# Two held operands of TensorE at a shifted address: cT by 256 bytes and dT by 384 bytes, in a two-layer hybrid trunk with experts

## The reference

```
for layer in (0, 1):
    h = rms_norm(x, mix_norm[layer])
    a, b, p, gc, gp = split(h @ w_in[layer])              # 1024 -> 3584 columns
    yc = silu(layer_norm(causal_conv31(a * sigmoid(b)))) @ w_conv_out[layer]
    yp = (sliding means of p over 2, 4, 8, 16 tokens - p) @ w_pool[layer] * pool_scale[layer]
    x = x + (sigmoid(gc) * yc + sigmoid(gp) * yp) @ w_out[layer]
    h = rms_norm(x, ffn_norm[layer])
    if layer == 0:  x = x + (silu(h @ w_gate) * (h @ w_up)) @ w_down           # width 2816
    else:           x = x + the two best of 8 experts of the same form, width 3584, weighted
return rms_norm(x, final_norm)
```

## Time and profile before

| what | value |
|---|---|
| median of three runs | 1425.84 us (1425.17 to 1426.02) |
| the profiled execution, its own time | 1425.18 us |
| its span in the profile | 1423.6 us |
| TensorE matmuls / weight loads | 6506 / 6506 |
| TensorE busy | 1409.4 us, 99% of the span |
| mean granted clock of TensorE, share of full speed | 0.998 |
| VectorE, ScalarE, GpSimd busy | 1174.7, 986.9, 207.9 us |
| memory traffic | 445.96 MB, 313 GB/s over the span |

### The profile page before, as it was taken

One profiled execution on the slowest core, in us unless ns is written; L12 is line 12 of the kernel. 1 busy time (PEld: TensorE's weight loads), 2 busy tenths in 40 slices (PEclk: granted clock), 3 DMA queues, 4 the chain that ended last, 5 costly groups with the idle time before them and its releaser, 6 DMA issues.

```text
span 1423.6 us, 18360 instructions
## 1 busy us (share of the span) xinstructions
PE 1409.4 (99%) x6506; PEld 1168.6 (82%) x6506; DVE 1174.7 (83%) x1068; ACT 986.9 (69%) x876; POOL 207.9 (15%) x249
## 2 busy tenths in 40 slices
PE   9999999999999999999999999999999999999997
PEld 7888888888888888888888888888888888888885
DVE  6987544548987998889899898888989989888896
ACT  7765444347765877867877777786787777778674
POOL 6840000005831001001001001000100100100010
PEclk9999999999999999999999999999999999999999
DMA  9656555545548899999999999999999999999990
GB/s 359 222 169 215 178 181 198 183 162 196 175 164 310 283 386 378 371 370 409 375 382 372 390 367 371 388 370 369 412 372 384 370 391 366 371 389 373 366 411 33
DMA packets 197552, 445.96 MB, mean 313 GB/s; under 512 B 8400, under 2 KB 19968, under 8 KB 197504
## 3 DMA queue, kind: packets, MB, share of 16 engines
q1 hardware_dynamic: 192496, 432.57, 80.4%
q0 software_dynamic: 2304, 8.39, 2.2%
q10 hardware_dynamic: 2704, 4.38, 0.9%
HBM read 437.97 MB, written 7.34 MB: 313 GB/s over the span
## 4 chain that ended last, share of the span: by engine, by line
issue 58%; PE 34%; POOL 4%; DVE 2%; ACT 1%; DMA 0%; POOLq 0%; ACTq 0%; DVEq 0%
PE bank L1467 10%; PE bank L1469 10%; PE bank L1468 10%; POOL small L611 2%; POOL gates L614 2%; DVE w_lo L989 1%; POOL sums L621 1%; PE bank L1528 1%; DVE bank L1038 1%; PE bank L1631 0%; PE bank L1593 0%; ACT w_hi L654 0%; PE bank L1763 0%; PE bank L1587 0%; DVE tokA L1104 0%
## 5 line engine op out<-in xcount | busy, mean ns | idle before, releaser
L989 DVE TENSOR_TENSOR w_lo<-raw,w_hi 128x2048 fp32r<-128x2048 f32 x256 | 582.9, 2292 | 134.8 <-ACT w_hi L654 134.6
L654 ACT ACTIVATE w_hi<-raw 128x2048 fp32r<-128x2048 f32 x256 | 488.6, 1913 | 200.2 <-PE bank L1469 199.8
L1467 PE MATMUL bank<-w_hi,dT_hi 128*128 128x512 f32 (+1 forms) x756 | 296.4, 392 | 0.0
L1469 PE MATMUL bank<-w_hi,dT_lo 128*128 128x512 f32 (+1 forms) x756 | 293.2, 388 | 0.0
L1468 PE MATMUL bank<-w_lo,dT_hi 128*128 128x512 f32 (+1 forms) x756 | 292.6, 387 | 0.0
L1467 PE MATMUL bank<-w_hi,cT_hi 128*128 128x512 f32 x492 | 194.3, 395 | 0.0
L1469 PE MATMUL bank<-w_hi,cT_lo 128*128 128x512 f32 x492 | 191.7, 390 | 0.0
L1468 PE MATMUL bank<-w_lo,cT_hi 128*128 128x512 f32 x492 | 191.6, 390 | 0.0
L1469 PEld LDWEIGHTS bank<-w_hi,dT_lo 128*128 128x128 f32 x756 | 142.0, 188 | 29.4
L1467 PE MATMUL bank<-w_hi,hT_hi 128*128 128x512 f32 x416 | 164.4, 395 | 1.1 <-DVE w_lo L1086 1.0
L1468 PEld LDWEIGHTS bank<-w_lo,dT_hi 128*128 128x128 f32 x756 | 142.2, 188 | 28.1
(11 more groups left out here) (256 smaller groups left out, 1865.8 us busy)
## 6 DMA issues: line engine op xcount, KB each, us to landing
raw<-in_moe_w_gate_dram SPq DMA_DIRECT2D x96, 1024.0 KB, 7.5
raw<-in_moe_w_up_dram SPq DMA_DIRECT2D x72, 1024.0 KB, 10.3
raw<-in_moe_w_down_dram SPq DMA_DIRECT2D x72, 1024.0 KB, 8.9
raw<-in_w_in_dram SPq DMA_DIRECT2D x20, 1024.0 KB, 7.1
mix<-in_moe_w_up_dram SPq DMA_DIRECT2D x16, 1024.0 KB, 8.8
gates<-in_moe_w_down_dram SPq DMA_DIRECT2D x16, 1024.0 KB, 11.3
gates<-in_moe_w_up_dram SPq DMA_DIRECT2D x16, 1024.0 KB, 8.8
work<-in_moe_w_down_dram SPq DMA_DIRECT2D x16, 1024.0 KB, 11.5
```

What stands on the lines that cost most here:

```text
L654: act.activation(w_hi[split_place(u, seen.item is not None)][:, 0:width], place[slot][:, 0:width], ACT.Copy).then_inc(hi_ready, 1)
L989: dve.tensor_tensor(w_lo[split][:, 0:width], place[slot][:, 0:width], w_hi[split][:, 0:width].bitcast(F32), ALU.subtract).then_inc(lo_read ...
L1467: nc.tensor.matmul(dst, a_hi, b_hi, start=start, stop=False)
L1469: return nc.tensor.matmul(dst, a_lo, b_hi, start=False, stop=stop)
```

## The change

Buffers are named in another order, and one unused buffer is added. `rw` moves from the end of the list to its front, `vecs` and `items` move from the front to just before `cT`. The bytes ahead of `raw` stay the same (256 + 64 + 64 for 224 + 64 + 32 + 64), so `raw`, `w_hi`, `w_lo`, `hT` and all that lies up to `y_lo` keep their addresses. `cT_hi` and `cT_lo` begin 256 bytes later than before, which is 256 past a multiple of 512. `to_384` adds 128 bytes more, so `dT_hi` and `dT_lo` begin 384 past a multiple of 512, and so do `row_gain`, `ident`, `mean_w` and `mix`; `taps` moves by 384 and the last small buffers by 128. The list now ends at 229288. No instruction is added, removed or moved.

```
@@ -230,9 +230,8 @@
-        vecs = sb("vecs", [P, 56])
+        rw = sb("rw", [P, KD, E])
         small = sb("small", [P, 16])
-        items = sb("items", [P, 8], I32)
         sb("to_512", [P, 16])
         raw = sb("raw", [P, RAW, UNIT])
@@ -252,8 +251,11 @@
         y_hi, y_lo = sb("y_hi", [P, D], F32R), sb("y_lo", [P, D], F32R)
+        vecs = sb("vecs", [P, 56])
+        items = sb("items", [P, 8], I32)
         cT_hi = sb("cT_hi", [P, CC * S], F32R)
         cT_lo = sb("cT_lo", [P, CC * S], F32R)
+        sb("to_384", [P, 32])
         dT_hi = sb("dT_hi", [P, GROUPS * S], F32R)
         dT_lo = sb("dT_lo", [P, GROUPS * S], F32R)
@@ -267,7 +269,6 @@
         taps = sb("taps", [P, 2, 124])
-        rw = sb("rw", [P, KD, E])
```

## The result

The changed kernel takes 1441.21 us (median of four, 1440.66 to 1441.9) against 1425.93 for the kernel before in the same comparison: a ratio of 1.0102, interval 1.0088 to 1.0115, or +15.3 us. The profiled execution has a span of 1439.7 us where it was 1423.6.

A forecast was written before the change was run, and what follows sets the result against it. TensorE's matmul spacing was taken to bound the kernel, everything ahead of it being early. All parts summed to 0 us on the profiled 1425.18 us; with the runs' median 0.66 us higher, the forecast was 1425.8 us, range 1388 to 1450.

The forecast's parts named there:

- Parts 1, 3, 4 and 5: Unchanged instructions; moved ident, mean_w, row_gain; mix as loading place and split source; moved vecs, items, rw, taps: 0 us each.
- part 2: cT 256 and dT 384 bytes on against unmoved streams, 4560 matmuls: spacing stays 226.7 ns, +0 us (bounds -53.4 to +37.8).
- one lost cycle per 16 bytes loaded: Reading of the 13.3 ns extra per large matmul as 32 cycles for a 512-byte held block, wherever the buffers lie.
- the strongest sign: Unsteady steps behind four transposes, ten averaging 231.0 ns and two of 235, with the same buffers as in steady stretches.
- the case without it: The forecast itself: distance has no meaning for the large matmuls, spacing stays 226.7 ns; 1425.8 us, chance 0.40.
- Rival B: Distance 0 is a good place; shifted cT and dT matmuls stay at 231.0 ns, +19.6 us, 1445 us; chance 0.25.
- The objection to it: Argument against the slower side: in the unsteady steps behind the transposes time is shifted, and no address; no size.
- Rival A: Distance 0 is a bad place for cT and dT matmuls; losing half the extra gives -27 us, 1399 us; chance 0.35.
- parts 2 and 3: Estimates for cT and dT matmuls and for transposes and means, both using 1.7 ns extra of a full float32 matmul.
- If an address matters at all, it is by its last 9 bits: In steady stretches, distances of 0 and 512 past a multiple of 1024 cost the same 226.7 ns per step.
- The rule of the Trainium skill: TensorE's two independent read ports let the next held operand load without taking bandwidth from the running matmul: 0 us.

The follow-up runs named there:

- e2_rest_only: The change with cT and dT put back at multiples of 512, only row_gain, ident, mean_w and mix still 384 past one: 1425.84 us, ratio 0.9998 to the kernel before.
- e6_both_256: The change without the 128 bytes of to_384, so cT and dT both at distance 256: 1426.09 us, ratio 1.0000 to the kernel before.
- e3_streams_128: Kernel before with streamed buffers and hT moved to 128 past a multiple of 512, cT and dT unmoved, both at distance 384: 1451.27 us, ratio 1.0175.
- e9_who_meets: Kernel before with test matmuls added behind its end, offsets alternating, then other widths and full float32; alternating offsets gave steps of 228.2 to 230.0 ns; no total given.

## Why the prediction was wrong

**The bound was read rightly.** TensorE's spacing set the end, nothing ahead of it was late, and every ns per matmul showed: step times count, with the counts of the prediction, gives 14.8 us for a median that rose by 15.3. Parts 1, 3, 4 and 5 hold: e2_rest_only and e6_both_256 put all of them together at 0 within 0.1%.

**The step that failed is part 2,** "The value that I take is 226.7, no change". For cT at 256 it is right. For dT at 384 the measured step is 232.4 in an undisturbed stretch, and the part that was put at +0 us is +14.8 us. I had put down the reason for "no change" as one lost cycle per 16 bytes loaded, which fitted two widths of stream and was never tested against the width of the load; held blocks of 96, 64 and 32 columns refute it (230.0 to 231.7 ns where it gives 223.3 to 216.7). Why the spacing depends on the distance stays open. The rows of before held better evidence: the earlier trace rows show steps of up to 235 ns with the same buffers, so the spacing is no constant. The prediction called this the strongest sign that the address could matter and then gave the forecast to the case without it.

**Rival B had the right direction and a close size.** It said that distance 0 is the good place and that a shifted held block would leave the spacing at the mean of the unsteady steps. The spacing does stay unsettled; that this comes from load and stream meeting, as B has it, no run shows, and the steps at 384 are not those behind the transposes. It priced that at 231.0 ns on all 4560 matmuls, +19.6 us; it was 232.4 on the 2784 that hold dT, and nothing on the other 1776. What it lacked is the period: 256 is as good as 0, so one of the two moved buffers cost nothing. The objection to it, that in those rows time is shifted and no address, did not hold it back: both count, as distance 16 shows. The longest step was given as 235 and is 241.

**That the time lies between 1388 and 1450 is luck.** The upper end was to leave out spacings above 232 ns, and the measured one is above it. It is 1441 only because cT, at 256, happened to cost nothing; e3_streams_128, where cT and dT both pay, is at 1451.3, outside.

**Rival A is refuted for these matmuls.** In 17 distances on the 16-byte grid, their repeats up to 480 and four distances off the grid none is below 226.65 ns. The 215.0 ns of the float32 record (215.7 over the 63 steps above, so its extra is nearer to 2.4 than to the 1.7 ns of parts 2 and 3) was reached at no distance. At 256 columns of `F32R` distance 0 is the worse place, by 1.4 ns; the kernel has few such matmuls.

**"If an address matters at all, it is by its last 9 bits"** held as far as tried: the last 8 bits of the distance set the steps.

**The rule of the Trainium skill** ("TensorE: Matmul & The Clock Gate", Part 2: What happens when you issue a matmul), by which loading the next held operand takes nothing from the running matmul, gave 0 us and was wrong here by 15.3. The runs do not show which read takes what from which, so the two ports themselves are not refuted; but a matmul's spacing depends on where the held operand lies against the streamed one, at 512 columns of `F32R`.

## What to carry to other kernels

When matmuls with 128 held columns run back to back at 512 columns of `F32R`, lay held and streamed buffers out so that their addresses differ by a multiple of 256 bytes; every other distance tried here cost 0.7 to 3.3% of each matmul at least at some starts, but for 272, which was tried from one start alone. It shows in no wait of TensorE, only in the distance between starts. For other widths measure: at 256 columns 128 was the better distance. Small buffers named between large ones set this distance by accident, and a few bytes of padding repair it. Where a trace shows that a cost varies from one matmul to the next for the same buffers, don't take the settled value for what a moved buffer will cost, and don't judge a layout by stretches that are all entered in the same way.

## What the runs showed of the hardware that I had not expected

- Spacing of 512-column `F32R` matmuls against distance: 226.7 ns at multiples of 256 bytes, 228.8 to 234.2 at the other multiples of 32, repeating every 256 bytes. The loss at distance 128 was 5.5 ns at 512 columns, 1.1 at 448, 2.2 at 384, 0 at 320 and -1.4 at 256. Full float32 of 256 columns has 215.7 ns per record at 0 and at 128.
- Steps fall into repeating patterns of unequal steps, at 384 one of seven (241, 232, 231, 232, 228, 230, 233) and, in e3_streams_128, another of 229 or 230 and 237 or 238 by turns. At distance 16 two patterns exist, 226.7 and 233.3, in the same kernel.
- At distance 0 with 128 held columns the step is columns / 2.4 plus 13.3 ns at 256, 320, 384 and 512 columns, and plus 16.0 at 448; it doesn't fall with the width of the held block. At distance 128 and 256 columns it is plus 11.9.
- In e9_who_meets the granted clock fell from 1.00 to 0.50 of full speed, the level of 1.2 GHz, at 1513 us, behind 17 us of matmuls with 128 and 64 columns (and 12 us of 256 columns before them), in which the profile shows TensorE and its weight loads busy without a gap. It was back at 1.00 at 1526.8 us, within full float32 matmuls of 256 columns. The stretch of 64 columns at distance 128 ran in it at 213 ns a step for 112 and says nothing on the distance. Here is that fall in the view by windows (stretch, its length, then busy us and counts of PE, PEld, DVE, ACT and POOL, then the clock):

```profile
1500.00:1512.90 12.90, 12.90 (x119) 12.90 (x118) 0.00 (x0) 0.00 (x0) 0.00 (x0) 1.00 0.00 1
1513.50:1523.50 10.00, 10.00 (x50) 10.00 (x48) 0.00 (x0) 0.00 (x0) 0.00 (x0) 0.50 0.00 0
```
